# Halves of the factor sums ahead of the last tile, and the first gain vector on SP's queue

## What is computed

```python
def rms_norm(x, g):
    y = xf * lax.rsqrt(jnp.mean(xf * xf, axis=-1, keepdims=True) + EPS)
    return (y * g.astype(jnp.float32)).astype(x.dtype)
...
    for l in range(DEPTH):
        h = rms_norm(x, norm_mix[l])
        ...
        x = x + jnp.concatenate([att, sgu], axis=-1) @ w_o[l]
        h = rms_norm(x, norm_ffn[l])
        x = x + jnp.square(jax.nn.relu(h @ w_up[l])) @ w_down[l]
    return rms_norm(x, norm_final)
```

## Time and profile before

| | before |
|---|---|
| time, median of 3 runs | 950.86 us (948.45 to 953.03) |
| profiled execution: time | 949.33 us |
| profiled execution: span | 947.4 us |
| granted TensorE clock, mean | 0.994 |
| TensorE, matmuls | 930.3 us, 98% |
| VectorE | 707.8 us, 75% |
| ScalarE | 563.8 us, 60% |
| GpSimd | 204.8 us, 22% |

### The profile page before, as it was taken

How to read it: one execution, slowest core, us unless ns; L and a number is a source line. 1 busy time by engine, 2 the same in 40 slices (tenths; PEclk the granted TensorE clock), 3 DMA queues, 4 the chain that set the end, 5 groups by cost and what they waited for, 6 DMA issues and landing times.

```text
span 947.4 us, 14055 instructions
## 1 busy us (share of the span) xinstructions
PE 930.3 (98%) x5632; PEld 819.0 (86%) x5632; DVE 707.8 (75%) x813; ACT 563.8 (60%) x843; POOL 204.8 (22%) x136
## 2 busy tenths in 40 slices
PE   8999999989999999999999999999899999999997
PEld 5888889978998998899888887899689989989985
DVE  5685525999779869879948752478987897798697
ACT  5556517775576376457655574377645756754764
POOL 2554224110011101011146433240101101101010
PEclk9999999999999999999999999999999999999999
DMA  9442150677668676676543320518668666676772
GB/s 292 127 135 71 42 150 28 167 166 206 147 171 204 134 232 134 178 190 156 165 150 134 112 68 23 155 24 245 139 173 205 149 198 158 161 198 150 205 156 89
DMA packets 40497, 141.76 MB, mean 150 GB/s; under 512 B 5616, under 2 KB 5744, under 8 KB 40432
## 3 DMA queue, kind: packets, MB, share of 16 engines
q1 hardware_dynamic: 28624, 98.32, 30.9%
q0 software_dynamic: 11520, 41.95, 25.3%
q10 hardware_dynamic: 288, 0.59, 0.2%
HBM read 138.74 MB, written 2.10 MB: 149 GB/s over the span
## 4 chain that ended last, share of the span: by engine, by line
PE 89%; DVE 6%; DMA 2%; ACT 1%; issue 1%; POOL 0%; DVEq 0%
PE bank L578 15%; PE bank L579 14%; PE bank L580 14%; PE bank L581 13%; PE bank L583 13%; PE bank L582 13%; DVE wlo L1316 2%; DMA raw<-weights_in 2%; PE bank L605 1%; PE bank L833 1%; PE bank L781 1%; DVE raw L1593 1%; PE bank L816 1%; PE bank L826 1%; PE bank L807 1%
## 5 line engine op out<-in xcount | busy, mean ns | idle before, releaser
L938 ACT ACTIVATE whi<-raw 128x1024 fp32r<-128x1024 f32 x268 | 281.0, 1057 | 165.2 <-PE bank L580 81.2
L1316 DVE TENSOR_TENSOR wlo<-raw,whi 128x1024 fp32r<-128x1024 f32 x218 | 264.8, 1223 | 79.8 <-ACT whi L938 79.4
L581 PE MATMUL bank<-xhi,wlo 128*128 128x256 f32 (+1 forms) x672 | 208.8, 311 | 0.0
L583 PE MATMUL bank<-xlo,whi 128*128 128x256 f32 (+1 forms) x672 | 207.3, 309 | 0.0
L582 PE MATMUL bank<-xhi,whi 128*128 128x256 f32 (+1 forms) x672 | 207.2, 308 | 0.0
L578 PE MATMUL bank<-wlo,fhi 128*128 128x512 f32 x448 | 176.3, 393 | 7.8 <-DVE flo L1580 7.8
L550 POOL DMA_DIRECT2D raw<-weights_in x80 | 69.4, 868 | 509.8 <-DVE raw L1593 236.0
L537 POOL TENSOR_TENSOR wlo<-raw,whi 128x1024 fp32r<-128x1024 f32 x50 | 135.2, 2714 | 195.4 <-ACT whi L938 195.4
L579 PE MATMUL bank<-whi,fhi 128*128 128x512 f32 x448 | 175.8, 392 | 0.0
L580 PE MATMUL bank<-whi,flo 128*128 128x512 f32 x448 | 175.5, 392 | 0.0
L581 PEld LDWEIGHTS bank<-xhi,wlo 128*128 128x128 f32 x672 | 128.3, 191 | 6.8 <-issue 0.3
(11 more groups left out here) (131 smaller groups left out, 1240.7 us busy)
## 6 DMA issues: line engine op xcount, KB each, us to landing
raw<-weights_in SPq DMA_DIRECT2D x172, 512.0 KB, 4.3
raw<-weights_in POOLq DMA_DIRECT2D x80, 512.0 KB, 6.1
xt<-x_in SPq DMA_DIRECT2D x4, 512.0 KB, 8.3
gbc<-gains_in SPq DMA_DIRECT2D x4, 512.0 KB, 4.3
out_t<-xt SPq DMA_DIRECT2D x3, 512.0 KB, 2.6
gbc<-gains_in ACTq DMA_DIRECT2D x1, 512.0 KB, 5.8
bias<-alibi_in SPq DMA_DIRECT2D x2, 256.0 KB, 7.3
wst<-ws_in SPq DMA_DIRECT2D x2, 256.0 KB, 7.0
```

The source lines that it names most:

```text
L581: pe.matmul(o, wlo[:, s, wc], hi[:, tokens], start=first, stop=False, skip_group_check=on_sum)
L583: return pe.matmul(o, whi[:, s, wc], lo[:, tokens], start=False, stop=last, skip_group_check=on_sum)
L938: act.activation(whi[:, n % SLOTS, :], raw_at(slot), ACT.Copy).then_inc(whi_ready, 1)
L1316: dve.tensor_tensor(wlo[:, n % SLOTS, :], raw_at(raw_slot(n)), whi[:, n % SLOTS, :], ALU.subtract) \
```

## The change

- `xs_make(i)` over all 256 columns becomes `xs_make(i, k)` over one half, `tok(k)`. The halves k = 0 move forward: S3's goes between turned_low(2) and normed(3), the other three between normed(3) and turned_low(3). The halves k = 1 stand where the whole sums stood. A half 0 waits for `xf_ready` of tile 2, a half 1 for that of tile 3; `made_x` gives the counts, and ScalarE's `xs_high` waits for half 1 of its sum.
- In quarter 0, `make(q, 0)` moves ahead of the low part of the second weight tile of the down product M1. In the other quarters it stays where it was.
- The gain vector of the first norm is loaded from SP's queue, behind the first tile of x and ahead of the first weight tile; ScalarE's queue no longer issues it.

```diff
--- before.py
+++ after.py
@@ -180,6 +180,11 @@
 def made_count(l, q, i):
 
     return (l * QUARTERS + q) * 4 + i + 1
+
+
+def made_x(l, i, k):
+
+    return l * 8 + 4 * k + i + 1
 
 
 def split_x(norm, i, b):
@@ -489,7 +494,10 @@
                     sp.dma_start(bsb[r * HD:(r + 1) * HD, :, :].rearrange("p c i -> p (c i)"), src) \
                         .then_inc(gate_landed, 16)
 
-            for t in range(NT):
+            load_x(0)
+            load_gain(0)
+            load_mix(0, 0)
+            for t in range(1, NT):
                 load_x(t)
                 load_mix(0, t)
             sp.dma_start(bias[:, :, :].rearrange("p c k -> p (c k)"), alibi).then_inc(const_landed, 16)
@@ -965,7 +973,6 @@
                     if norm % 2 == 0 or i < 2 or b:
                         act.copy(xhi[:, 4 * b:4 * b + 4, tok(t)], src).then_inc(xhi_ready, 1)
 
-            act.dma_start(gbc[:, :], gains[0:1, :].broadcast_to([P, D])).then_inc(gain_landed, 16)
             act.dma_start(ident[:, :], ident_in).then_inc(ident_landed, 16)
             act.wait_ge(eps_set, 1)
             act.activation(root[:, :], eps[:, 0:1], ACT.Sqrt)
@@ -1138,8 +1145,8 @@
 
                 def xs_high(i):
 
-                    made, src = ((1, s3), (3, xf[:, 0, :, :]), (2, xf[:, 3, :, :]), (4, xf[:, 1, :, :]))[i]
-                    act.wait_ge(xs_made, l * 4 + made)
+                    made, src = ((0, s3), (2, xf[:, 0, :, :]), (1, xf[:, 3, :, :]), (3, xf[:, 1, :, :]))[i]
+                    act.wait_ge(xs_made, made_x(l, made, 1))
                     act.copy(factor_x((S3, S2, S5, S4)[i])[0], src).then_inc(xs_hi, 1)
 
                 def copy_sum(q, r, h):
@@ -1513,30 +1520,34 @@
                     dve.tensor_tensor(xt[:, t, cols], bank(l, 4 * h + t)[:, :], xt[:, t, cols], ALU.add) \
                         .then_inc(x_added, 1)
 
+                def xs_make(i, k):
+
+                    x11, x12, x22, x21 = (xf[:, b, :, tok(k)] for b in range(4))
+                    if i == 0:
+                        dve.wait_ge(xf_ready, l * 2 * NT + 6 + 2 * k)
+                        dve.tensor_tensor(s3[:, :, tok(k)], x11, x21, ALU.subtract).then_inc(xs_made, 1)
+                    elif i == 1:
+                        dve.wait_ge(xs_made, made_x(l, 0, k))
+                        dve.tensor_tensor(x21, x22, x21, ALU.subtract).then_inc(xs_made, 1)
+                    elif i == 2:
+                        dve.wait_ge(xs_made, made_x(l, 1, k))
+                        dve.scalar_tensor_tensor(x11, x21, -1.0, x11, ALU.mult, ALU.subtract).then_inc(xs_made, 1)
+                    else:
+                        dve.wait_ge(xs_made, made_x(l, 2, k))
+                        dve.scalar_tensor_tensor(x12, x11, -1.0, x12, ALU.mult, ALU.subtract).then_inc(xs_made, 1)
+
                 for t in range(NT):
                     add(0, t)
                 for t in range(NT):
                     add(1, t)
                     if t:
                         turned_low(2 * l + 1, t - 1)
+                    if t == NT - 1:
+                        xs_make(0, 0)
                     normed(2 * l + 1, t)
+                for i in range(1, 4):
+                    xs_make(i, 0)
                 turned_low(2 * l + 1, NT - 1)
-
-                def xs_make(i):
-
-                    x11, x12, x22, x21 = (xf[:, b, :, :] for b in range(4))
-                    if i == 0:
-                        dve.wait_ge(xf_ready, (l + 1) * 2 * NT)
-                        dve.tensor_tensor(s3, x11, x21, ALU.subtract).then_inc(xs_made, 1)
-                    elif i == 1:
-                        dve.wait_ge(xs_made, l * 4 + 1)
-                        dve.tensor_tensor(x21, x22, x21, ALU.subtract).then_inc(xs_made, 1)
-                    elif i == 2:
-                        dve.wait_ge(xs_made, l * 4 + 2)
-                        dve.scalar_tensor_tensor(x11, x21, -1.0, x11, ALU.mult, ALU.subtract).then_inc(xs_made, 1)
-                    else:
-                        dve.wait_ge(xs_made, l * 4 + 3)
-                        dve.scalar_tensor_tensor(x12, x11, -1.0, x12, ALU.mult, ALU.subtract).then_inc(xs_made, 1)
 
                 def xs_low(i):
                     src = (s3, xf[:, 0, :, :], xf[:, 3, :, :], xf[:, 1, :, :])[i]
@@ -1619,13 +1630,13 @@
 
                 for q in range(QUARTERS):
                     if q == 0:
-                        xs_make(0)
+                        xs_make(0, 1)
                         low_up(q, M7, 0)
                         xs_low(0)
                         sum_m6(q, UP, 0)
                         low_up(q, M7, 1)
-                        xs_make(1)
-                        xs_make(2)
+                        xs_make(1, 1)
+                        xs_make(2, 1)
                         low_up(q, M6, 0)
                         xs_low(1)
                         sum_m6(q, UP, 1)
@@ -1638,7 +1649,7 @@
                         up_sum(q, M2, 1)
                         xs_low(2)
                         low_up(q, M5, 0)
-                        xs_make(3)
+                        xs_make(3, 1)
                         up_sum(q, M4, 0)
                         low_up(q, M5, 1)
                         up_sum(q, M4, 1)
@@ -1649,6 +1660,7 @@
                         low_up(q, M3, 1)
                         factor_low(q, M1)
                         low_down(q, M1, 0)
+                        make(q, 0)
                         low_down(q, M1, 1)
                     else:
                         low_up(q, M7, 0)
@@ -1675,7 +1687,7 @@
                         up_sum(q, M5, 0)
                         low_down(q, M1, 1)
                         up_sum(q, M5, 1)
-                    make(q, 0)
+                        make(q, 0)
                     low_down(q, M7, 0)
                     sum_m6(q, DOWN, 0)
                     factor_low(q, M7)
```

## The result

| | before | changed |
|---|---|---|
| median | 951.05 us (6 runs, 948.45 to 953.03) | 957.13 us (6 runs, 955.97 to 959.87) |
| ratio | | 1.0067, interval 1.0047 to 1.0087 |
| profiled execution: time, span | 949.33, 947.4 | 956.92, 955.0 |

What follows compares the result with a forecast made beforehand. TensorE, busy 930.3 of 947.4 us, bounds the kernel. Profiled 949.33, 0 for the gain vector and +5.3 for the sums give 954.6, 956.2 on the median's scale; 955.9 stated, 8-in-10 range 950.5 to 959.5.

Steps and rivals of the forecast that it cites:

- The meeting with GpSimd: Fourth tile's second norm: S3's half delays `hid` behind GpSimd's subtraction, TensorE stands still 2.95 us; +2.65 net per layer.
- rival 1: VectorE's `hid` gets in ahead of GpSimd's subtraction; TensorE waits 0.8 us, in all +1.3, 952.2 us; chance 19%.
- Rival 2: `hid` loses to GpSimd in one layer and goes first in the other; +3.3, 954.2 us; chance 12%.
- rival 3: The meeting costs nothing and all sums hide in VectorE's idle times; -0.6, 950.2 us; chance 8%.
- Who goes first: At `hid`, GpSimd's start 0.05 us ahead (0.04 in layer 1) would keep the port; no row settled so close a case.
- Rival 4: TensorE's stall for `hid` pulls the clock to 1.2 GHz: 1.7 us per layer; about a quarter of the forecast's 61%.
- the later stall: TensorE's wait at M6 in quarter 0, shortened from 3.7 to about 3.4 us, may at times lose its 1.7 us slow clock.
- The small gain later: Down phase before the stall at M6: 0.16 to 0.44 us gained per layer, 0.3 taken, 0.6 in all.
- The gain vector: Kernel start: x's first tile sooner, but TensorE's warm-up ends at 10.06; 0 taken, range -0.2 to +0.4 us.
- a sign of being wrong: For the gain vector's load: TensorE's first transposes near 10.1, or those at 14.2, coming later.

Runs made afterwards that it cites:

- the run with the quarter: Changed kernel with only half of S3's first half (128x256) ahead of normed(3), the other 128x256 behind it; 953.97 us, ratio 1.0020.
- the kernel with GpSimd out of the way: Changed kernel, all four first halves behind normed(3), low part of M2's second weight tile moved from GpSimd to VectorE; 951.31 us, ratio 0.9997.
- the longer measurement: Second run, in more rounds, of the kernel before with only the gain vector's load moved to SP's queue; 952.06 us, ratio 1.0005.

## Why the prediction was right

*The meeting with GpSimd.* The step that carried the forecast held in every part. S3's half: until 159.40 forecast, 159.60 measured, with 0.2 of start in it. `hid` starts 0.05 us behind GpSimd: 0.04. It lasts some 3.4: 3.40. What TensorE loses there: 2.95 forecast, 2.9 measured in both layers. The choice between the forecast and rival 1 was open by the rows. The changed kernel went the forecast's way in both layers, and the run with the quarter shows that rival 1 is the same mechanism with the other one first. Rival 2 (one layer each way) and rival 3 (the meeting costs nothing) didn't occur.

*Who goes first.* The Trainium skill, "SBUF — State Buffer", section "Who interferes with whom", has the one that is issued first keep the shared port for its whole instruction. The traces agree: GpSimd ahead by 0.04 us held `hid` off for its full 2.36, VectorE ahead by 0.25 held GpSimd off to 3.29.

*The slow clock.* Rival 4 occurred in one layer of two. In the changed kernel 1.00 is granted behind the wait of 2.75 and 0.50 behind the one of 2.74. The kernel without the moved `make` has it the other way round: 0.50 in layer 0, 1.00 in layer 1, with waits of 2.74 in both. The prediction had priced it at 1.7 us per layer, up to 959.6. It also expected the later stall to lose its slow clock at times because it is shorter, and that came too, in layer 1 of both kernels (waits of 3.44 and 3.56). But it comes with no shortening as well: it happened behind 3.65 in the kernel with GpSimd out of the way and behind 3.63 in the one with the quarter. In the two traces with the full loss, the slow stretches gained and lost are equal in number, so the net of the clock is nothing. Why one wait is followed by the slow clock and another isn't stays open.

*The small gain later.* 0.3 us per layer was taken for the down phase. It can't be found. The waits for D.M6, which were to fall to 3.3 to 3.5, are 3.65 and 3.44. In the profile it is buried under a weight landing that differs by up to 2 us between executions, and in the times of the kernel with GpSimd out of the way the interval of 0.2% each way, some 2 us, is three times the 0.6 looked for. The term is neither shown nor refuted.

*The gain vector.* 0 was taken, and the longer measurement says 1.0005. Its reason was only half right. In the changed kernel's profile the transposes come at 10.19 and 14.43 instead of 10.06 and 14.20, which the prediction had named as a sign of being wrong; it is 0.2 us, inside the -0.2 to +0.4 that it allowed. And the end of the warm-up isn't fixed at 10.06: in two traces with the gain vector moved TensorE turns the first tile at 8.65 and 8.69, for which the earlier tile is needed. What leaves nothing of it is the second tile, which comes no sooner and whose squares stand ahead of the first tile's cast.

*The size.* 6.1 measured against 5.0. The two waits give 5.8. The forecast took 0.6 off for the later gain and 0.3 for the clock. Neither is to be seen: the first is too small for these runs, and the second was offset by the slow clock behind a wait for `hid`. With an interval of 4.5 to 8.3 us on the measurement, how near the two numbers came is in part luck; the two waits aren't.

## What to carry to other kernels

An idle stretch in one engine's row is room only if the operation put there doesn't share something with another engine that is busy just then. Look at the operands: with two in SBUF on VectorE, beside a GpSimd subtraction as here, the one that started second waited for the other's end. Count this in twice: for the operation moved, and for the next critical one, which it may push just behind GpSimd's next start.

When two starts lie within a tenth of a microsecond and 3 us hang on the order, the order should be made certain, by giving the work to one engine or by moving the op out of the way.

## What the runs showed of the hardware that I had not expected

The exclusion acts over so small a lead as 0.04 us: `hid` at 159.76 against GpSimd's 159.72, and the whole of GpSimd's 2.36 us was waited for.

The granted clock after a wait is not a matter of the wait's length alone. It fell to 1.2 GHz behind waits of 3.65, 2.74, 2.41 and 2.34 us, and stayed at 2.4 GHz behind others of 3.65, 3.44, 2.75 and 2.38. The window behind the 3.65 us wait of layer 0 in the kernel with GpSimd out of the way:

```profile
213.00:214.00 1.00, 1.00 (x6) 0.82 (x5) 1.00 (x2) 0.00 (x0) 0.00 (x0) 1.00 1.09 193
```

The same load, in the same program, took 8.1 us in one execution and 9.7 in another. TensorE's waits of about a microsecond at D.M7 go with the long flights, in the kernel with only the gain vector moved (1.50) as well as in the changed one (1.18).
